# A mixture-of-experts kernel: expert items sorted by the table, and a second TensorE loop with 128 moving columns instead of 160

## The chip, the cores and the metric

One core of one Trainium2 chip runs the whole program. The metric is the device time in microseconds (us) of one execution; the time of a kernel is the median of its runs. Engine names are those of the profile: PE is TensorE's matmul side and PEld its weight loads, DVE is VectorE, ACT is ScalarE, POOL is GpSimd, SP is SyncE, which issues the weight loads.

## The reference, cut to what matters

The layer computes, for 1024 tokens of width 1024, a normalization, an input projection, two kinds of attention, an output projection, and then a mixture of experts. The change touches the last part alone.

```python
logits = (h @ w_router + b_router)
top_val, top_idx = lax.top_k(logits, 4)          # 4 of 32 experts per token
gate = jax.nn.softmax(top_val, axis=-1)
...
gu = xblk @ w_gate_up[e] + b_gate_up[e]
g_lin = jnp.minimum(gu[:, :D_EXPERT], 7.0)
u_lin = jnp.clip(gu[:, D_EXPERT:], -7.0, 7.0)
act = g_lin * jax.nn.sigmoid(1.702 * g_lin) * (u_lin + 1.0)
y = act @ w_down[e] + b_down[e]                  # times its gate, added to the token's row
```

Each expert has three 1024x1024 float32 matrices (gate, up, down), 12.58 MB. There are 4096 token-expert pairs, 128 per expert on average. Evaluated on the reference's inputs, the router gives the 32 experts these counts of tokens, in order of the expert's number: 128, 122, 123, 140, 105, 142, 107, 120, 131, 126, 127, 114, 147, 126, 138, 121, 120, 131, 118, 108, 160, 136, 132, 101, 121, 139, 112, 124, 129, 146, 152, 150. Fourteen are over 128 and none is over 160.

## The kernel before, in words

**Items.** The last block of the program (from L1125) works in items. An item is one expert and up to `SL` = 160 of its tokens; an expert with more would get a further item. A table in on-chip memory (`table`) holds for each item the expert and the first position; it is built at run time from the counts, on DVE and PE (L1442 to L1460 and L1620 to L1633). The first 32 entries are the experts in the order of their numbers, so item 0 is expert 0, whose weights are loaded before the table is there. `count_items` (L1121) loads the number of items on every engine, and every engine runs a loop over all items but the last (`Fori(0, n_last)`), then a copy of the loop's body for the last one.

**Tokens.** Tokens are the moving side of each product. DVE's `choose` (L1373) marks the tokens of an item, PE's `find` (L1543) turns the marks into row numbers, DVE's `rows` (L1379) into indices, and POOL gathers the rows (L1181), 80 in each of two halves. PE turns them (`turn_x`, L1551), ACT copies the result as a high and a low float16 part (`x_split`, L1249). Places without a token point at spare rows behind the output and have a gate of zero.

**Weights.** An item's weights come in six chunks of 2 MB: chunks 0 and 1 are the halves of gate, 2 and 3 of up, 4 and 5 of down. Three raw buffers make a ring: SP issues the load of chunk m+3 when DVE has finished with chunk m (`item_loads`, L1137). ACT writes a chunk's high float16 part (`high_part`, L1244, the instruction is L1247), DVE its low part (`low_part`, L1409, the instruction is L1412), into a ring of three part buffers, which ACT may fill again when PE has used them. Chunks 6 and 7 are chunks 0 and 1 of the next item.

**Products.** For every 128x128 piece of a weight chunk, `product` (L1577) issues three matmuls (high by high, high by low, low by high), each with its own weight load and 160 moving columns. A chunk is 96 matmuls, an item 576. I call an item's six products G0, G1, U0, U1, D0 and D1. PE's order in an item (L1643) is G0, `find` of the next item, two turns of the previous item's result (`turn_y`, L1563), G1, two more, U0, U1, half of the next item's `turn_x`, D0, the other half, D1. G0 writes the banks that hold D1's result of the item before, so its first three tiles wait until ACT has copied three tiles of that result (`y_copy`, L1279).

**DVE's order** in an item (L1468): `shift`, `rows` of the next item, low part 2, three `gate_read`, low part 3, five `gate_read`, low part 4, `gate_act`, the activation (`activate`, `activate_low`, L1424 to L1438), low part 5, `bias`, low part 6, `choose`, low part 7. **ACT's order** (L1294): high part 2, y rows, high part 3, y rows, high part 4, sigmoids, high part 5, `up_read` with activation parts, half of `x_split`, high parts 6 and 7, the other half, `y_copy`. All engines take their instructions strictly in this written order.

Of the kernel before, what the change touches and what calls it, by code (L numbers as in the profile page):

```python
# [6 lines left out]
BF16 = mybir.dt.bfloat16  # L7
FP16 = mybir.dt.float16
I32 = mybir.dt.int32
ALU = mybir.AluOpType  # L10
# [12 lines left out]
def build_trunk(nc, x, norm1_g, w_in, sb_q_norm_g, sb_k_norm_g, sb_out_norm_g, hg_lb_logits,  # L23
# [14 lines left out]
    with ExitStack() as ctx:  # L38
# [847 lines left out]
        ITEMS = NE + T * TOPK // SL  # L886
# [124 lines left out]
        table = sb("table", [1, 2 * TAB + 2], I32)  # L1011
        MORE = MAXC - 1
        work = region_b[:, 8192 + 6 * D:8192 + 8 * D]
# [15 lines left out]
        code_e, thr, pos1 = take(1), take(MORE), take(MORE)  # L1029
        code16 = take(4).bitcast(BF16)  # L1030
        over = take(4).bitcast(BF16)[:, 0:MORE]
        hot = take((MORE * TAB + 1) // 2).bitcast(BF16)[:, 0:MORE * TAB].rearrange("p (c j) -> p c j", c=MORE)
# [8 lines left out]
        NP8 = 15  # L1041
# [82 lines left out]

        with nc.Block() as block:  # L1125
# [29 lines left out]
            def _(pool):  # L1155
# [16 lines left out]
                pool.tensor_copy(code16[:, 1:1 + MORE], thr).then_inc(s_p8, 3)  # L1172
# [164 lines left out]
            def _(dve):  # L1337
# [95 lines left out]
                def activate_low(i, q):  # L1433
# [16 lines left out]
                link(dve.scalar_tensor_tensor(out=pos1[0:NE, :], in0=bank[4][0:NE, 0:MORE], scalar=float(NE + 1), in1=over[0:NE, :],  # L1450
                                              op0=ALU.add, op1=ALU.mult))
                dve.tensor_tensor(hot[0:NE, :, :], iota[0:NE, 1:TAB + 1].unsqueeze(1).to_broadcast([NE, MORE, TAB]),
                                  pos1[0:NE, :].unsqueeze(2).to_broadcast([NE, MORE, TAB]), ALU.is_equal).then_inc(s_hot, 1)
                dve.tensor_scalar(table[:, 2 * TAB:2 * TAB + 1], bank[4][0:1, MORE:MORE + 1], float(NE), None, ALU.add)
                dve.tensor_scalar(table[:, 2 * TAB + 1:2 * TAB + 2], bank[4][0:1, MORE:MORE + 1], float(NE - 1), None, ALU.add)
# [3 lines left out]
                dve.tensor_copy(table[:, NE:TAB], bank[3][0:1, NE:TAB])  # L1459
                dve.tensor_copy(table[:, TAB:2 * TAB], bank[3][0:1, TAB:2 * TAB]).then_inc(s_table, 1)  # L1460
# [62 lines left out]
            def _(pe):  # L1523
# [53 lines left out]
                def product(out_ap, r, f, kk, k, hi, lo, first):  # L1577
# [5 lines left out]
                def gate(i, half):  # L1583
                    pe.wait_ge(s_lod, i * CH + (half + 1))
                    for f in range(KT):
                        if half == 0 and f % TPB == 0:
                            pe.wait_ge(s_dnc, i * 3 + (f // TPB + 1))
                        for kk in range(HK):
                            if f == 0 and kk == 0:
                                pe.wait_ge(s_xhi, i * 2 + (half + 1))  # L1590
                                pe.wait_ge(s_xlo, i * 2 + (half + 1))
                            mm = product(tile_at(0, f), half, f, kk, half * HK + kk, xT_hi, xT_lo, half == 0 and kk == 0 and f % TPB == 0)
                        mm.then_inc(s_g, 1)

                def up(i, half, last):
# [3 lines left out]
                    for f in range(KT):  # L1599
                        for kk in range(HK):  # L1600
                            mm = product(tile_at(3, f), (2 + half) % RING, f, kk, half * HK + kk, xT_hi, xT_lo,
# [3 lines left out]
                def down(i, half):  # L1605
                    pe.wait_ge(s_lod, i * CH + (4 + half + 1))
                    for k0, k1 in ((0, 2), (2, 4)) if half == 0 else ((0, 4),):
                        for f in range(KT):
                            if half == 0 and k0 == 0 and f % TPB == 0:
                                pe.wait_ge(s_gev, i * 8 + min(f + TPB, KT))  # L1610
                            for kk in range(k0, k1):
# [4 lines left out]
                                mm = product(tile_at(0, f), (4 + half) % RING, f, kk, k, aT_hi, aT_lo, k == 0 and f % TPB == 0)  # L1616
# [5 lines left out]
                pe.matmul(bank[4][0:NE, 0:MORE], lt16[0:NE, 0:NE], over[0:NE, :], start=True, stop=False, skip_group_check=True)  # L1622
# [65 lines left out]
```

## Time and profile before

| What | Value |
|---|---|
| median of 3 runs | 2249.86 us (2248.14 to 2250.61) |
| the profiled execution, its own time | 2252.61 us |
| its span in the trace | 2250.7 us |
| mean granted TensorE clock over the span | 0.964 |
| PE busy | 2116.3 us, 94% of the span |
| DVE busy | 1548.6 us, 69% |
| ACT busy | 1412.7 us, 63% |
| POOL busy | 604.2 us, 27% |
| moved by DMA | 489.40 MB, mean 217 GB/s |

Shares are averages over a program with very different stages: up to about 800 us the attention part runs, with few loads; from then on the items. A matmul's busy time includes its way through a pipeline, so the time from one to the next has to be taken from a run of many, not from the mean of one. A timeline row gives the start, the length up to the end of the last instruction it merges, the engine, the line and the operation, and in brackets how long the engine stood idle before it and what ended that.

### The profile page before, as it was taken

The page shows a single profiled execution, that of the slowest core. Times are in us where ns is not written, and L with a number is a line of the kernel's source. Part 1 is how long each engine was busy: PE and PEld are TensorE (multiplying, and loading weights), DVE is VectorE, ACT ScalarE, POOL GpSimd, SP SyncE. Part 2 cuts the span into 40 slices and gives each one's busy share as a digit, 9 for nine tenths or more (in the row PEclk, how much of TensorE's full clock was granted, in tenths as well). Part 3 has the DMA queues.
Part 4 walks back from the last instruction along what each step waited for, and adds up shares of the span by engine and source line. Part 5 has one row for each costly group of instructions (what it writes and reads, how often), then busy time and mean ns, then how long its engine had stood idle before and what let it go on. Part 6 is the DMA issues. An engine that isn't in the chain of part 4 may idle for free.

```text
span 2250.7 us, 59693 instructions
## 1 busy us (share of the span) xinstructions
PE 2116.3 (94%) x24537; PEld 1796.4 (80%) x24537; DVE 1548.6 (69%) x1933; ACT 1412.7 (63%) x1633; POOL 604.2 (27%) x379
## 2 busy tenths in 40 slices
PE   5999999999937958999999999999999999999998
PEld 3444864344813548999999999999999999999997
DVE  5331424444673247888888888888888888888886
ACT  4331315564263346787777778778777877877884
POOL 2221212222050122322332332242233224223221
PEclk7999999999958969999999999999999999999999
DMA  4111100000031267898898998989889898988987
GB/s 159 38 46 48 57 1 1 0 1 1 30 121 50 84 238 260 311 326 315 316 327 306 329 316 315 328 314 328 307 317 326 311 334 313 329 308 317 325 307 239
DMA packets 142564, 489.40 MB, mean 217 GB/s; under 512 B 12794, under 2 KB 27898, under 8 KB 142448
## 3 DMA queue, kind: packets, MB, share of 16 engines
q1 hardware_dynamic: 129648, 444.78, 54.0%
q0 software_dynamic: 12864, 43.88, 8.2%
q8 instruction: 38, 0.62, 0.1%
q14 instruction: 14, 0.11, 0.0%
HBM read 457.34 MB, written 35.52 MB: 219 GB/s over the span
## 4 chain that ended last, share of the span: by engine, by line
PE 57%; DVE 3%; DMA 2%; issue 1%; ACT 1%; POOL 0%; POOLq 0%; DVEq 0%; SPq 0%; ACTq 0%
PE banks L1580 52%; PE banks L1574 3%; DVE region_c L1412 2%; PE banks L1560 1%; DMA rows_out<-region_b 1%; PE banks L1547 1%; DMA region_d<-w_down_dram 0%; DMA region_b<-rows_out,region_d 0%; ACT region_b L1267 0%; DMA rows_out<-region_b,region_d 0%; DVE region_b L1438 0%; ACT region_b L1253 0%; ACT region_b L1263 0%; POOL rows_out L1185 0%; POOL region_b L1177 0%
## 5 line engine op out<-in xcount | busy, mean ns | idle before, releaser
L1580 PE MATMUL banks<-region_b,region_c 128*128 128x160 f16 x18432 | 1300.1, 233 | 8.6 <-DVE region_c L1412 5.9
L1580 PEld LDWEIGHTS banks<-region_b,region_c 128*128 128x128 f16 x18432 | 1281.3, 98 | 12.9 <-DVE region_c L1412 7.0
L1412 DVE TENSOR_TENSOR region_c<-region_a,region_c 128x4096 f16<-128x4096 f32 x128 | 565.5, 4418 | 28.5 <-ACT region_c L1247 14.4
L1247 ACT ACTIVATE region_c<-region_a 128x4096 f16<-128x4096 f32 x128 | 462.5, 3613 | 52.1 <-DMA region_a<-w_gate_up_dram 52.1
L1181 POOL DMA_INDIRECT region_b<-rows_h,region_d x64 | 294.3, 4598 | 35.8 <-issue 28.8
L1247 ACT ACTIVATE region_c<-region_d 128x4096 f16<-128x4096 f32 x64 | 231.5, 3618 | 100.6 <-DMA region_d<-w_gate_up_dram 63.8
L1412 DVE TENSOR_TENSOR region_c<-region_d,region_c 128x4096 f16<-128x4096 f32 x64 | 282.5, 4414 | 2.7 <-ACT region_c L1247 2.7
L1190 POOL TENSOR_TENSOR region_d<-region_d 80x1 f32<-80x1 f32 x96 | 20.2, 210 | 923.6 <-DVE region_d L1389 656.8
L345 PE MATMUL banks<-region_a,region_d 128*128 128x512 f16 x960 | 210.9, 382 | 7.8 <-POOL region_d L319 7.8
L345 PEld LDWEIGHTS banks<-region_a,region_d 128*128 128x128 f16 x960 | 94.6, 99 | 124.3 <-POOL region_d L319 8.2
L1276 ACT ACTIVATE region_b<-banks,region_d 80x512 f32<-80x512 f32 x128 | 80.4, 678 | 138.8 <-PE banks L1574 125.7
L265 ACT ACTIVATE region_d<-region_d 128x2048 f16<-128x2048 f32 x14 | 26.6, 1909 | 147.9 <-PE banks L345 114.2
L1185 POOL DMA_INDIRECT rows_out<-region_b,region_d x66 | 100.3, 1520 | 43.5 <-issue 22.4
L319 POOL TENSOR_TENSOR region_d<-region_d 128x2048 f16<-128x2048 f32 x14 | 57.0, 4074 | 201.3 <-ACT region_d L265 201.3
L400 DVE COPY region_b<-banks 128x512 f32<-128x512 f32 x32 | 22.1, 692 | 127.9 <-PE banks L345 127.9
L513 DVE TENSOR_SCALAR region_a<-banks 128x1024 f32<-128x1024 f32 (+3 forms) x48 | 46.0, 958 | 91.4 <-PE banks L581 60.7
L1284 ACT ACTIVATE region_b<-banks,b_dcur 128x160 f32<-128x160 f32 x256 | 79.9, 408 | 23.4 <-PE banks L1580 23.1
L1263 ACT ACTIVATE region_b<-banks,region_d 128x160 f32<-128x160 f32 x256 | 85.1, 386 | 13.9 <-PE banks L1580 13.9
L972 PE MATMUL banks<-region_c,region_a 128*128 128x512 f16 x256 | 80.6, 387 | 11.2 <-DVEq L949 10.2
L550 ACT ACTIVATE region_a<-banks 128x1024 f32<-128x1024 f32 (+3 forms) x48 | 38.9, 810 | 77.9 <-PE banks L595 76.5
L353 PE MATMUL banks<-region_d,region_a 128*128 128x256 f16 x768 | 84.0, 273 | 0.0
L353 PEld LDWEIGHTS banks<-region_d,region_a 128*128 128x128 f16 x768 | 75.1, 98 | 8.9
(246 smaller groups left out, 2214.9 us busy)
## 6 DMA issues: line engine op xcount, KB each, us to landing
region_a<-w_gate_up_dram SPq DMA_DIRECT2D x192, 1024.0 KB
region_d<-w_gate_up_dram SPq DMA_DIRECT2D x64, 1024.0 KB
region_a<-w_down_dram SPq DMA_DIRECT2D x64, 1024.0 KB
region_d<-w_down_dram SPq DMA_DIRECT2D x64, 1024.0 KB
region_d<-w_in_dram SPq DMA_DIRECT2D x14, 1024.0 KB, 5.0
region_b<-x_dram SPq DMA_DIRECT2D x8, 1024.0 KB, 8.7
region_c<-w_out_dram SPq DMA_DIRECT2D x8, 512.0 KB, 3.6
rows_out<-region_b SPq DMA_DIRECT2D x8, 512.0 KB, 2.7
```

The costliest lines, as they stand in the source:

```text
L345: mm = pe.matmul(bank[q][:, :], a, b, start=(k == 0 and j == 0), stop=(k == KT - 1 and j == 2))
L353: mm = pe.matmul(bank[q][:, tt * WC:(tt + 1) * WC], a, b, start=(k == 0 and j == 0), stop=(k == KT - 1 and j == 2))
L972: mm = pe.matmul(bank[half][:, :], a, b, start=(k == 0 and j == 0), stop=(k == KT - 1 and j == 2))
L1181: pool.indirect_dma_start(out=xg[:, h, :], out_offset=None, in_=rows_h2[:, :], in_offset=bass.IndirectOffsetOnAxis(ap=rows_get[:, h:h + 1] ...
L1185: pool.indirect_dma_start(out=rows_out[:, :], out_offset=bass.IndirectOffsetOnAxis(ap=rows_prev[:, h:h + 1], axis=0), in_=yrow[:, h, :], i ...
L1247: act.activation(part_hi[r], raw[r], ACT.Copy).then_inc(s_hi9, 1)
L1263: act.activation(u_all[:, f * SL:f * SL + SL], tile_at(3, f), ACT.Identity, bias=b_cur[:, KT + f:KT + f + 1]).then_inc(s_uev, 1)
L1276: act.activation(yrow[:, h, q * 512:q * 512 + 512], bank[Y_BANK[g]][0:HS, :], ACT.Copy, scale=gate_prev[:, h:h + 1]).then_inc(s_yrow, 1)
L1284: ins = act.activation(yT[:, f, :], tile_at(0, f), ACT.Identity, bias=b_dcur[:, f:f + 1])
L1412: dve.tensor_tensor(part_lo[r], raw[r], part_hi[r], ALU.subtract).then_inc(s_lod, 1)
L1574: mm = pe.transpose(bank[Y_BANK[g]][0:HS, d * P:d * P + P], yT[:, 4 * q + d, h * HS:h * HS + HS], ident[:, :])
L1580: mm = pe.matmul(out_ap, a, b, start=(first and s == 0), stop=(k == KT - 1 and s == 2), skip_group_check=True)
```

## The change

Both the table and PE's code change. The table now lists first expert 0 (its threshold is set to -1, so that it always counts) and the experts with over 128 tokens, then further items of experts with over 160, then the experts with 128 or fewer. It is built from eight kinds of entry instead of six, each with a product of its own, and `table` gets one more word, the number of wide items. PE loads that number (`count_wide`), runs a loop over the wide items with 160 moving columns, a second loop with 128, and the last item with 128. The tiles keep their distance of 160 columns, and all other engines keep their loops and their 160 columns, so that DVE and ACT read 32 columns per tile that a narrow item's products do not write. DVE's `choose` of item 1 now takes its expert from the table, after the wait for it.

```diff
-        ITEMS = NE + T * TOPK // SL
+        ITEMS = NE + T * TOPK // SL + 2
+        NARROW = P
...
+        KINDS = MORE + 2
...
+        def count_wide(eng):
+            return eng.value_load(table[0:1, 2 * TAB + 2:2 * TAB + 3], min_val=1, max_val=ITEMS - 2)
...
-                pool.iota(thr, [[SL, MORE]], base=SL, channel_multiplier=0, allow_small_or_imprecise_dtypes=True).then_inc(s_p8, 1)
-                pool.wait_ge(s_p8, 10)
+                pool.iota(thr[:, 1:MORE + 1], [[SL, MORE]], base=SL, channel_multiplier=0, allow_small_or_imprecise_dtypes=True).then_inc(s_p8, 1)
+                pool.memset(thr[:, 0:1], float(NARROW)).then_inc(s_p8, 1)
+                pool.wait_ge(s_p8, 11)
+                pool.affine_select(out=thr[:, 0:1], in_=thr[:, 0:1], compare_op=ALU.is_gt, fill=-1.0, base=0, pattern=[[0, 1]],
+                                   channel_multiplier=1).then_inc(s_p8, 1)
...
-                dve.tensor_tensor(over[0:NE, :], thr[0:NE, :], bank[3][0:NE, 0:1].to_broadcast([NE, MORE]), ALU.is_lt).then_inc(s_over, 1)
+                dve.tensor_tensor(over[0:NE, 0:MORE + 1], thr[0:NE, :], bank[3][0:NE, 0:1].to_broadcast([NE, MORE + 1]), ALU.is_lt)
+                dve.tensor_tensor(over[0:NE, MORE + 1:KINDS], thr[0:NE, 0:1], bank[3][0:NE, 0:1], ALU.is_ge).then_inc(s_over, 1)
...
-                link(dve.tensor_copy(table[:, 0:NE], iota[0:1, 0:NE]))
...
-                dve.tensor_scalar(table[:, 2 * TAB:2 * TAB + 1], bank[4][0:1, MORE:MORE + 1], float(NE), None, ALU.add)
-                dve.tensor_scalar(table[:, 2 * TAB + 1:2 * TAB + 2], bank[4][0:1, MORE:MORE + 1], float(NE - 1), None, ALU.add)
+                link(dve.tensor_copy(totals[0:1, :], bank[4][0:1, KINDS - 1:KINDS + 1]))
+                dve.tensor_copy(table[:, 2 * TAB + 2:2 * TAB + 3], totals[0:1, 0:1])
+                dve.tensor_scalar(past[0:1, :], iota[0:1, 0:TAB], totals[0:1, 1:2], float((MAXC - 1) * SL), ALU.is_ge, ALU.mult)
+                link(dve.scalar_tensor_tensor(out=n_all[0:1, :], in0=totals[0:1, 0:1], scalar=2.0, in1=totals[0:1, 1:2],
+                                              op0=ALU.add, op1=ALU.max))
+                dve.tensor_copy(table[:, 2 * TAB:2 * TAB + 1], n_all[0:1, :])
+                dve.tensor_scalar(table[:, 2 * TAB + 1:2 * TAB + 2], n_all[0:1, :], -1.0, None, ALU.add)
...
-                choose(1, 0)
                 dve.wait_ge(s_table, 1)
+                choose(dve.value_load(table[0:1, 1:2], min_val=0, max_val=NE - 1),
+                       dve.value_load(table[0:1, TAB + 1:TAB + 2], min_val=0, max_val=(MAXC - 1) * SL))
...
-                def product(out_ap, r, f, kk, k, hi, lo, first):
+                def product(tile, width, r, f, kk, k, hi, lo, first):
+                    out_ap, hi, lo = tile[:, 0:width], hi[:, :, 0:width], lo[:, :, 0:width]
...
-                with pe.Fori(0, n_last) as i:
-                    item(i, False)
-                item(n_last, True)
+                n_wide = count_wide(pe)
+                with pe.Fori(0, n_wide) as i:
+                    item(i, False, SL)
+                with pe.Fori(n_wide, n_last) as i:
+                    item(i, False, NARROW)
+                item(n_last, True, NARROW)
```

## Rows read from the trace of the kernel before

**Rows 1.** The page's first part: busy time of each engine.
```profile
PE 2116.3 (94%) x24537; PEld 1796.4 (80%) x24537; DVE 1548.6 (69%) x1933; ACT 1412.7 (63%) x1633; POOL 604.2 (27%) x379
```

**Rows 2.** The chain that ended last, two items: start, length, what.
```profile
1709.86 13.42 PE banks L1580 x192
...
1732.29 13.28 PE banks L1580 x192
...
1753.36 13.38 PE banks L1580 x192
```

**Rows 3.** Waits from 880 to 2180 us by engine: total us, times, longest.
```profile
PE banks L1580 <- DVE region_c L1412: 0.7, 4, 0.2
...
DVE region_d L1384 <- PE banks L1547: 107.0, 30, 3.6
...
ACT region_c L1247 <- DMA region_d<-w_gate_up_dram: 61.7, 30, 2.3
```

**Rows 4.** Windows: us; busy us of PE, PEld, DVE, ACT, POOL; clock, DMA share, GB/s.
```profile
1622.70:1666.20 43.50, 43.47 (x640) 43.31 (x640) 37.44 (x44) 33.91 (x38) 13.06 (x7) 1.00 0.91 319
```

**Rows 5.** The page's costliest groups: products with 160 and with 256 moving columns.
```profile
L1580 PE MATMUL banks<-region_b,region_c 128*128 128x160 f16 x18432 | 1300.1, 233 | 8.6 <-DVE region_c L1412 5.9
...
L353 PE MATMUL banks<-region_d,region_a 128*128 128x256 f16 x768 | 84.0, 273 | 0.0
```

**Rows 6.** Timeline of one item, 1709 to 1754 us.
```profile
1709.12 0.74 PE L1560 MATMUL banks<-region_d,region_b 80*128 80x80 f16 x16
...
1709.84 4.42 DVE L1412 TENSOR_TENSOR region_c<-region_a,region_c 128x4096 f16<-128x4096 f32 x1
1709.94 0.93 SPq L1062 DMA_DIRECT2D region_d<-w_gate_up_dram  x2
1709.94 3.62 ACT L1247 ACTIVATE region_c<-region_a 128x4096 f16<-128x4096 f32 x1 [1.57 <-DMA region_a<-w_gate_up_dram]
...
1714.64 1.82 ACT L1284 ACTIVATE region_b<-banks,b_dcur 128x160 f32<-128x160 f32 x6
...
1719.26 3.62 ACT L1247 ACTIVATE region_c<-region_d 128x4096 f16<-128x4096 f32 x1 [1.90 <-DMA region_d<-w_gate_up_dram]
...
1723.12 0.74 PE L1547 MATMUL banks<-values,region_b 128*80 128x6 bf16 x16
...
1723.99 0.17 DVE L1384 COPY region_d<-banks 80x12 f32<-80x12 f32 x1 [3.57 <-PE banks L1547]
...
1724.86 4.41 DVE L1412 TENSOR_TENSOR region_c<-region_d,region_c 128x4096 f16<-128x4096 f32 x1
...
1729.43 0.93 SPq L1062 DMA_DIRECT2D region_d<-w_down_dram  x2
...
1738.96 3.62 ACT L1247 ACTIVATE region_c<-region_d 128x4096 f16<-128x4096 f32 x1 [0.97 <-PE banks L1580]
...
1743.18 0.33 DVE L1427 TENSOR_SCALAR region_b<-region_b 128x320 f32<-128x320 f32 x1 [0.45 <-ACT region_b L1263]
...
1753.03 3.62 ACT L1247 ACTIVATE region_c<-region_a 128x4096 f16<-128x4096 f32 x1 [1.20 <-DMA region_a<-w_gate_up_dram]
```

**Rows 7.** One window of 1 us in that item, columns as in rows 4.
```profile
1729.00:1730.00 1.00, 1.00 (x17) 1.00 (x15) 1.00 (x4) 0.14 (x1) 1.00 (x1) 1.00 0.00 0
```

**Rows 8.** Timeline, 800 to 885 us: table's last write, first low part, first shift.
```profile
822.17 0.20 DVE L1460 CAST table<-banks 1x65 int32<-1x65 f32 x1
...
824.95 4.42 DVE L1412 TENSOR_TENSOR region_c<-region_a,region_c 128x4096 f16<-128x4096 f32 x1 [2.58 <-ACT region_c L1247]
...
852.27 0.17 DVE L1400 COPY region_d<-region_d 80x2 f32<-80x2 f32 x1 [15.06 <-DMA rows_out<-region_b,region_d]
```

**Rows 9.** Timeline of the end, 2140 to 2251 us.
```profile
2242.48 1.41 DVE L1519 SCALAR_TENSOR_TENSOR region_b<-banks,region_d,region_b 80x512 f32<-80x512 f32 x2 [11.36 <-DMA region_b<-rows_out,region_d]
```

**Rows 10.** Timeline and clock of the first item: products after pauses of PE.
```profile
857.99 14.86 PE L1580 MATMUL banks<-region_b,region_c 128*128 128x160 f16 x192 [3.34 <-DVE region_c L1412]
...
875.31 6.80 PE L1580 MATMUL banks<-region_b,region_c 128*128 128x160 f16 x96 [1.88 <-DVE region_b L1438]
```

More of the change, by code:

```diff
@@ L1040, in build_trunk @@
         s_gissue = sem("first_gather_issued")
-        NP8 = 15
+        NP8 = 17
         CH = 6
@@ L1581, in product, with gate @@
                     return mm
-                def gate(i, half):
+                def gate(i, half, width):
                     pe.wait_ge(s_lod, i * CH + (half + 1))
@@ L1591, in gate, with up @@
                                 pe.wait_ge(s_xlo, i * 2 + (half + 1))
-                            mm = product(tile_at(0, f), half, f, kk, half * HK + kk, xT_hi, xT_lo, half == 0 and kk == 0 and f % TPB == 0)
+                            mm = product(tile_at(0, f), width, half, f, kk, half * HK + kk, xT_hi, xT_lo, half == 0 and kk == 0 and f % TPB == 0)
                         mm.then_inc(s_g, 1)
-                def up(i, half, last):
+                def up(i, half, last, width):
                     pe.wait_ge(s_lod, i * CH + (2 + half + 1))
@@ L1615, in down @@
                                     pe.wait_ge(s_alo, i * 4 + (k // 2 + 1))
-                                mm = product(tile_at(0, f), (4 + half) % RING, f, kk, k, aT_hi, aT_lo, k == 0 and f % TPB == 0)
+                                mm = product(tile_at(0, f), width, (4 + half) % RING, f, kk, k, aT_hi, aT_lo, k == 0 and f % TPB == 0)
                             if k1 == 4:
@@ L1621, in _ @@
                 pe.wait_ge(s_over, 1)
-                pe.matmul(bank[4][0:NE, 0:MORE], lt16[0:NE, 0:NE], over[0:NE, :], start=True, stop=False, skip_group_check=True)
-                for c in range(MORE):
-                    mm = pe.matmul(bank[4][0:NE, c + 1:MORE + 1], ones16[0:NE, 0:NE], over[0:NE, c:c + 1].to_broadcast([NE, MORE - c]),
-                                   start=False, stop=(c == MORE - 1), skip_group_check=True)
+                pe.matmul(bank[4][0:NE, 0:KINDS], lt16[0:NE, 0:NE], over[0:NE, :], start=True, stop=False, skip_group_check=True)
+                for c in range(KINDS):
+                    mm = pe.matmul(bank[4][0:NE, c + 1:KINDS + 1], ones16[0:NE, 0:NE], over[0:NE, c:c + 1].to_broadcast([NE, KINDS - c]),
+                                   start=False, stop=(c == KINDS - 1), skip_group_check=True)
                 mm.then_inc(s_upto, 1)
                 pe.wait_ge(s_hot, 1)
-                for c in range(MORE):
+                for c in range(KINDS):
                     pe.matmul(bank[3][0:1, 0:TAB], code16[0:NE, 0:1], hot[0:NE, c, :], start=(c == 0), stop=False, skip_group_check=True)
                 for c in range(MORE):
-                    mm = pe.matmul(bank[3][0:1, TAB:2 * TAB], code16[0:NE, 1 + c:2 + c], hot[0:NE, c, :], start=False, stop=(c == MORE - 1),
+                    mm = pe.matmul(bank[3][0:1, TAB:2 * TAB], code16[0:NE, 1 + c:2 + c], hot[0:NE, c + 1, :], start=False, stop=(c == MORE - 1),
                                    skip_group_check=True)
@@ L1641, in _, with item @@
                 n_items, n_last = count_items(pe)
-                def item(i, last):
-                    gate(i, 0)
+                def item(i, last, width):
+                    gate(i, 0, width)
                     if not last:
```

35 lines of the change are left out of this document (18 added, 17 removed).

## The prediction

> **What bounds the kernel now.** The page's first part puts PE at 94% of the span, far ahead of DVE, ACT and POOL [rows 1]. That is an average, and a busy PE need not be the limit, so I look next at the chain that ended last. From 880 us on it is nearly all item products; the same place in two neighbouring items, D1 with G0 behind it, begins at 1709.86 and at 1753.36, a period of 43.50 us [rows 2]. The table of waits agrees: over 1300 us the products waited 0.7 us for their weights, while DVE waited 107.0 us (30 times 3.6) for PE's `find`, and ACT 61.7 us for loads [rows 3]. So PE sets the pace, and the reader should see how narrowly: in one item DVE is busy for 37.44 us, ACT for 33.91, and the DMA engines for 0.91 of 43.50, which is 39.6 us [rows 4]. The counts in the section on the reference, and the 18432 products = 32 times 576 [rows 5], say that there are 32 items. With expert 0 and the 14 experts over 128 tokens, 15 are wide after the change and 17 narrow.
>
> **PE's part of a narrow item.** 192 products of 160 columns take 13.28 us, 69.2 ns each [rows 2]. 768 of 256 columns, each with its own weight load too, take 84.0 us, 109.4 ns each [rows 5]. That is 0.42 ns per column, so 128 columns should take 55.8 ns: an item saves 576 times 13.4 ns = 7.7 us, and PE alone would need 43.5 - 7.7 = 35.8 us. Could the weight load set a floor between? The lower bound of the rows is 16 products of 80 columns with a weight load of 128 columns each: 0.74 us less the 0.20 that one lasts, over 15, is 36 ns [rows 6]. The upper bound is 69.2 ns, no gain. I take 55.8, since 160 and 80 columns both scale with the columns. The Trainium skill speaks against the change here: its page "TensorE: Matmul & The Clock Gate", section "Back-to-back issue gap", has a stream of weight load and matmul at about 81 ns each for 128 columns. By it a narrow item would cost 576 times 11.8 ns = 6.8 us more and the kernel about 2366 us; the trace disagrees already, since 160 columns with the same load run at 69.2 ns.
>
> **What is late next.** If PE needs 35.8 us, DVE's 37.4 and the loads come ahead of it. The order of work is fixed, so I follow the two loops that the next item hangs on, with the durations of rows 6.
>
> *Loop A, through chunk 2.* Its load is issued when low part 5 ends, at 1709.84, and ACT can start on it at 1719.26 (9.4 us). High part and step to DVE: 3.7. So low part 2 can start 13.1 us after D1's start; now it starts at 1724.86, 15.0 after. From there to the end of low part 5 (1753.2) are 28.4 us, of which PE's share goes: the 0.97 that ACT's high part 5 waits for U0, the 0.45 that the activation waits for ACT because of it, and I count 0.4 for shorter waits of the kind inside the activation. Loop A: 13.1 + 28.4 - 1.8 = 39.7 us.
>
> *Loop B, through chunk 7.* Chunk 5's load is issued at 1729.43; chunk 7 is used at 1753.03, and the DMA engines work without a pause between. That is 23.6. Behind it ACT does the high part and two x copies (1709.94 to 1714.64: 4.7) and three y copies (0.9), without which G0 can't start. Then G0, 96 times 55.8 ns = 5.4; `find` to DVE (1723.12 to 1723.99) 0.9; `rows` 0.9; low part 2 and the issue 4.6. Sum 41.0 us. Now the same loop is 42.3, inside 43.5. It may shrink by up to 1.1: the gather of the next item's rows moves up into chunk 4's time, and chunk 7 is issued some 0.8 us sooner after chunk 6, as a pause of the queue shows that it waits for issues, not for bandwidth [rows 7].
>
> So a narrow item takes between 39.7 and 41.0; I take 40.5, nearer the loop that is the longer. That saves 3.0 us in each of 16 items. The last one loads no chunks 6 and 7; I give it 2. PE then stands idle for 4 to 5 us of each narrow item, ahead of D0 and D1.
>
> **Start.** The table gains two kinds of entry (four small matmuls) and six small DVE instructions against one removed, at the 0.20 us of its last write at most [rows 8]; with the matmuls I count 1.5 us. It was written at 822.37 and DVE's next big step began at 824.95, when ACT's first high part was ready [rows 8]: a cover of 2.6 us. POOL's two more small instructions (again 0.2 each) come ahead of the clearing of the spare rows and its store. The first item then waits until 852.27 for two scatters behind that store [rows 8]; the store lies in SP's queue behind 6 MB of weight loads, so I take 0 and keep 0.4. The two values loaded before `choose` of item 1 and PE's `count_wide` are some 0.1 us each; `choose` is covered by G0, PE's by that same wait till 852 us. If all of the cover were gone the start would cost 2 us in all.
>
> **Loop change and end.** Entering the last item's own copy of the code costs PE nothing now; entering a second loop should not either, bounds 0 and 1 us. Table order only changes which expert's weights come when; the bytes are the same. The bound at the end is a gather of the last rows, released by DVE after the last low part; it is awaited until 2242.48 [rows 9], so a shorter last D1 brings nothing.
>
> **Sum.** 16 times 3.0 and 2 is 50 us, less 1 for start and loop change: 49. Against the profiled execution's 2252.6 us that is 2203.6; the median of the runs is 2.7 us lower, so I predict **2201 us**, own range 2190 to 2212 (per item 39.7 to 41.0, and the loop change).
>
> **Rivals.**
> (1) *The loads hold more than I think.* If the DMA engines' 39.6 busy us don't shrink and half of the 3.9 us without traffic stays (the wait for low part 5, ahead of chunk 2), an item takes 41.6: saving 17 times 1.9 = 32, time 2218; with scatters in the way of chunk 2 up to 2230. For it: a share of 0.91 [rows 4]. Against it: pauses with nothing in flight [rows 7]. Chance 0.20.
> (2) *DVE alone sets the pace.* Loads land earlier once they are issued more evenly, and an item takes 37.4 + 1 of waits = 38.5: 85 us less, 2165 (PE's own floor would give 2119). Against it: ACT already waits 2 us per item for chunk 2 [rows 3]. Chance 0.10.
> (3) *No gain*, because the weight load's pace is 69 ns or the sort puts nothing into the narrow loop (the change doesn't do what it says): 2250. The rows with 80 and 256 columns speak against the first, the counts against the second. Chance 0.04.
> (4) *Slower: the clock falls.* PE now runs without pauses and the granted clock is 1.00 [rows 4]. After a pause of 3.34 us in the first item, 192 products took 14.86 us, not 13.45; after one of 1.88 us, 96 took the usual 6.80 [rows 10]. A narrow item has pauses of about 2.6 us (before D0) and 1.4 (before D1). If each cost 1.4 us, PE would need 38.6 us and nothing changes; it decides only from 7.7 us lost per item, 144 products at half the clock. With half of the products there (288 times 53 ns = 15.3), an item takes 51 and the kernel 17 times 7.6 = 129 us more, 2379. Chance 0.03.
>
> **How the numbers follow.** My case has 0.63, the rivals 0.20, 0.10, 0.04 and 0.03. The range of 8 in 10 takes my case and most of (1) and part of (2): 2176 to 2225. What this kernel's measurement can tell from no change is about 0.2%, 4.5 us. Faster: my case, (1) and (2), 0.93. Same: (3), 0.04. Slower: (4), 0.03.
>
> **What would show it.** Right: 9792 products with 128 columns (17 times 576) and 8640 with 160; 96 of 128 columns in about 5.4 us; periods of 43.5 us in the first 15 items and 40 to 41 afterwards; `find` no longer awaited for 3.6 us by DVE; new waits of PE before D0 and D1 for DVE; a granted clock still at 1.00; the first item's G1 and U0 where they were. Wrong: products 69 ns apart (3), the DMA share near 1.00 and ACT's waits for chunks grown (1), wide items slower than 43.5, or a clock below 1 in the narrow part (4).

## The result and the profile after

The changed kernel takes 2218.91 us (median of 4 runs, 2216.3 to 2220.97) against 2249.14 for the kernel before beside it: a ratio of 0.9866, with an interval of 0.9851 to 0.9882. That is faster by 30 us. The range of 8 in 10 (2176 to 2225) held it, the likeliest case's own range (2190 to 2212) did not: 48 us were forecast. It came out at the time worked out for rival (1), 2218.

The profiled execution took 2216.3 us, with a span of 2214.5, so 2.6 us under the median, where the one of before lay above its own. Its page first, the busy engines and the costliest groups:

```profile
PE 2010.8 (91%) x24541; PEld 1685.8 (76%) x24541; DVE 1547.2 (70%) x1937; ACT 1409.8 (64%) x1633; POOL 610.6 (28%) x381
...
L1190 POOL DMA_INDIRECT region_b<-rows_h,region_d x64 | 298.8, 4668 | 35.8 <-issue 28.8
```

PE lost 105 us of work [rows 1], DVE and ACT next to none (1.4 and 2.9 us), and the kernel gained less than a third of that. The line of the products is L1596 now; with its shapes kept apart (busy us, mean ns, idle before it):

```profile
L1596 PE MATMUL banks<-region_b,region_c 128*128 128x160 f16 x8640 | 611.6, 233 | 6.9 <-DVE region_b L1447 2.9 <-issue 2.1 <-DVE region_c L1421 1.2
L1596 PE MATMUL banks<-region_b,region_c 128*128 128x128 f16 x9792 | 579.3, 223 | 65.3 <-DVE region_b L1447 37.4 <-ACT region_b L1293 18.7 <-DVE region_c L1421 9.0
```

9792 products are narrow and 8640 wide, so 17 items and 15. Of the 72 us that PE waits ahead of products, 65 lie in the narrow items. The chain that ended last has a wide item, a narrow one in which the clock was low for a while (products at 1732.37, granted clock 0.64 on average over them), and two narrow ones at the full clock:

```profile
1054.39 13.46 PE banks L1596 x192
...
1732.37 8.32 PE banks L1596 x96
...
1741.27 5.36 PE banks L1596 x96
...
1787.92 5.52 PE banks L1596 x96
...
1811.27 12.13 DMA region_a<-w_gate_up_dram
...
1829.39 5.52 PE banks L1596 x96
```

In the wide part the chain was all products; now a load of some 12 us stands in most narrow items, and in a few one of 8 us for chunk 5. The period of a narrow item is 1829.39 - 1787.92 = 41.47 us. From `find` to `find` the 14 last narrow periods take 41.42 on average, two at the change of loops 42.4 and 42.5, and the first 12 wide ones 43.60, against 43.50 for the same 12 before. One wide window and two narrow ones, columns as in rows 4:

```profile
1100.00:1143.50 43.50, 43.50 (x645) 43.48 (x643) 37.76 (x45) 34.13 (x38) 13.05 (x7) 1.00 0.90 321
1751.00:1793.00 42.00, 37.06 (x657) 36.48 (x655) 37.42 (x44) 34.62 (x38) 13.27 (x7) 1.00 0.95 339
1793.00:1835.00 42.00, 36.87 (x655) 36.29 (x653) 37.44 (x44) 34.38 (x38) 13.39 (x7) 1.00 0.96 336
```

The wide one is that of [rows 4] again. In the narrow ones no engine is full, and the DMA share rose to 0.95 or 0.96: times 41.4 that is some 39.6 us of DMA work per item, what it was. The waits from 880 to 2150 us (total, times, longest):

```profile
DVE region_d L1393 <- PE banks L1562: 89.4, 30, 4.9
...
ACT region_c L1256 <- DMA region_d<-w_gate_up_dram: 54.9, 30, 2.8
ACT region_c L1256 <- DMA region_a<-w_gate_up_dram: 45.6, 30, 2.7
...
PE banks L1596 <- DVE region_b L1447: 34.6, 16, 3.1
...
ACT region_c L1256 <- DMA region_d<-w_down_dram: 25.5, 14, 3.3
...
PE banks L1596 <- ACT region_b L1293: 17.1, 14, 1.6
```

Beside [rows 3]: PE now waits for DVE's activation in every narrow item (ahead of D0) and, which was not forecast, for ACT's y copies (ahead of G0). ACT's waits for the half of `w_down` that is chunk 5 grew to 25.5 us; in the kernel before the same view has 7.9 us for them, in 6 waits from 880 to 2180. DVE still waits for `find`. One narrow item in the timeline, from low part 2 to the next low part 2:

```profile
1795.12 4.42 DVE L1421 TENSOR_TENSOR region_c<-region_d,region_c 128x4096 f16<-128x4096 f32 x1
1795.65 4.72 POOL L1190 DMA_INDIRECT region_b<-rows_h,region_d  x1 [0.57 <-issue]
...
1799.71 0.93 SPq L1065 DMA_DIRECT2D region_d<-w_down_dram  x2
...
1808.63 3.62 ACT L1256 ACTIVATE region_c<-region_d 128x4096 f16<-128x4096 f32 x1 [1.76 <-DMA region_d<-w_down_dram]
...
1815.01 5.52 PE L1596 MATMUL banks<-region_b,region_c 128*128 128x128 f16 x96 [2.12 <-DVE region_b L1447]
...
1822.57 5.53 PE L1596 MATMUL banks<-region_b,region_c 128*128 128x128 f16 x96 [1.46 <-DVE region_c L1421]
...
1822.67 0.93 SPq L1065 DMA_DIRECT2D region_d<-w_gate_up_dram  x2
1823.49 3.62 ACT L1256 ACTIVATE region_c<-region_a 128x4096 f16<-128x4096 f32 x1 [2.38 <-PE banks L1596]
...
1828.18 2.39 ACT L1293 ACTIVATE region_b<-banks,b_dcur 128x160 f32<-128x160 f32 x8
...
1829.39 5.52 PE L1596 MATMUL banks<-region_b,region_c 128*128 128x128 f16 x96 [1.29 <-ACT region_b L1293]
...
1834.74 0.74 PE L1562 MATMUL banks<-values,region_b 128*80 128x6 bf16 x16
...
1835.62 0.17 DVE L1393 COPY region_d<-banks 80x12 f32<-80x12 f32 x1 [2.46 <-PE banks L1562]
...
1836.59 4.42 DVE L1421 TENSOR_TENSOR region_c<-region_d,region_c 128x4096 f16<-128x4096 f32 x1
```

Both loops of the prediction can be measured here. Through chunk 7 (loop B of the prediction): issue of chunk 5 to high part 7, 1823.49 - 1799.71 = 23.8; to the start of the y copies 4.7; to G0 1.2 (three copies, and 0.24 until PE starts); to `find` 5.35; to DVE 0.9; `rows` 1.0; low part 2 and the issue 4.6: together 41.5, the item. (That high part names PE as what it waited for; PE's products were long done, and the chain has the load, 1811.27 and 12.13 us, ending there.) Through chunk 2 (loop A): 13.2 from the end of low part 5 to that of high part 2, then 27.4 from low part 2 to the end of low part 5: 40.6. Third is the DMA work, 39.6. Three limits lie within 2 us.

In time the change is this: 14 narrow periods less 2.1 each is 29.4, two of 1.0, the wide ones give back 1.2 in all, behind the last `find` 2.7, and the first shift comes 4 us sooner, at 848.00, of which 3 reach the first items [rows 8]. That is 36, the difference of the spans. The last 3 are the run's and not the change's: the kernel of run e8 below, which has no sort, has its first shift at 847.88.

```profile
823.07 4.43 DVE L1421 TENSOR_TENSOR region_c<-region_a,region_c 128x4096 f16<-128x4096 f32 x1 [0.40 <-issue]
...
848.00 0.17 DVE L1409 COPY region_d<-region_d 80x2 f32<-80x2 f32 x1 [13.96 <-DMA rows_out<-region_b,region_d]
```

### The profile page after: what moved, and what is told of

Same layout as the page of the kernel before. It is cut to its first block, busy times and chain, and to the rows that moved or that the text cites. A ratio compares the mean times of both kernels' runs of the same rounds, so it can differ in the third digit from the quotient of the medians.

```text
span 2214.5 us, 59720 instructions
## 1 busy us (share of the span) xinstructions
PE 2010.8 (91%) x24541; PEld 1685.8 (76%) x24541; DVE 1547.2 (70%) x1937; ACT 1409.8 (64%) x1633; POOL 610.6 (28%) x381
## 4 chain that ended last, share of the span: by engine, by line
PE 31%; DMA 11%; DVE 10%; issue 8%; ACT 2%; SPq 0%; POOL 0%; DVEq 0%; ACTq 0%; POOLq 0%
PE banks L1596 28%; DVE region_c L1421 8%; DMA region_a<-w_gate_up_dram 7%; DMA region_d<-w_down_dram 2%; PE banks L1589 1%; DVE region_b L1426 1%; DMA rows_out<-region_b 1%; DMA region_d<-w_gate_up_dram 1%; PE banks L1562 1%; PE banks L1575 1%; ACT region_b L1262 1%; ACT region_b L1260 0%; SPq L1065 0%; DMA region_b<-rows_out,region_d 0%; ACT region_b L1293 0%
## 5 line engine op out<-in xcount | busy, mean ns | idle before, releaser
L1596 PE MATMUL banks<-region_b,region_c 128*128 128x128 f16 (+1 forms) x18432 | 1190.8, 228 | 72.1 <-DVE region_b L1447 40.3
L1596 PEld LDWEIGHTS banks<-region_b,region_c 128*128 128x128 f16 x18432 | 1171.6, 99 | 80.0 <-ACT region_b L1276 42.3
L1190 POOL DMA_INDIRECT region_b<-rows_h,region_d x64 | 298.8, 4668 | 35.8 <-issue 28.8
```

Source lines behind the costliest of these rows:

```text
L1190: pool.indirect_dma_start(out=xg[:, h, :], out_offset=None, in_=rows_h2[:, :], in_offset=bass.IndirectOffsetOnAxis(ap=rows_get[:, h:h + 1] ...
L1596: mm = pe.matmul(out_ap, a, b, start=(first and s == 0), stop=(k == KT - 1 and s == 2), skip_group_check=True)
```

## The experiments

What had to be told apart: is the narrow item held by its order (the loop through chunk 7), by the loads' bytes, by a clock that was granted at 0.96 of full in most narrow items, or does the sort cost something of its own? Each kernel was timed beside the kernel before. Edits are to the changed kernel unless said.

**e1, sort alone.**

```diff
-                    item(i, False, NARROW)
-                item(n_last, True, NARROW)
+                    item(i, False, SL)
+                item(n_last, True, SL)
```

> The change without its narrow products: the table is sorted and PE has its second loop, but both loops use 160 moving columns; the result is the reference's. If the sort, the larger table and the second loop cost next to nothing, as the prediction has it, the time is 2249 us within 3, and an item takes 43.5 us in both loops. If the 0.2 us that each wide item grew by in the changed kernel (43.7 against 43.5) come with the new code and not with the narrow items, all 32 items take 43.7 here and the time is 2252 to 2256 us, unless the start is shorter by the 3 us that it is in the changed kernel's profile.

Measured: 2251.51 us against 2248.97, ratio 1.0012 [1.0003, 1.0022]. The first shift came at 847.03, and an item of its second loop has the window of [rows 4]:

```profile
1676.43:1719.94 43.51, 43.51 (x643) 43.37 (x641) 37.58 (x44) 33.93 (x37) 13.12 (x7) 1.00 0.92 320
```

So table, sort and second loop cost 2.5 us, by the interval between 0.7 and 4.9; the gain is that of the columns alone.

**e2, 96 columns.** As e1's diff, with 96 in place of `NARROW`.

> The change with 96 instead of 128 moving columns in the narrow loop; tokens past the 96th of a narrow item are left out of the products. Theory A (the loop through chunk 7: loads of chunks 5 to 7, high part, x copies, y copies, G0, find, rows, low part 2): only G0's saving lies in the loop, 96 times 13.3 ns = 1.3 us, until the loop through chunk 2 (40.6 us in the changed kernel's trace) takes over: narrow items 40.6 instead of 41.4, time 2205 within 4. Theory B (the DMA engines' 39.6 us of work per item and a pause that stays): nothing changes, 2219. Theory C (PE still bounds, by its own speed or its clock): 7.7 us less per narrow item, below 2110.

Measured: 2232.84 us, 0.9921 [0.9901, 0.9941]: slower than with 128 columns, by 14 us. PE has less to do than with 128 columns, and most items are longer, 39.9 to 47.3 us, with a lower mean clock (0.926). Here is one of them:

```profile
1884.00:1928.50 44.50, 30.17 (x644) 29.35 (x641) 37.33 (x45) 33.72 (x37) 12.95 (x7) 0.88 0.90 308
```

PE is idle for 14 of 44.5 us, no engine is full, and the DMA share is down. Something gets in the way when PE is early.

**e3, the y copy first.** G0 waits for this copy; it is put ahead of an x copy that has time.

```diff
                         high_part(7, i * 64 + 96)
+                    y_copy(i, 0)
+                    if not last:
                         x_split(i + 1, 1)
-                    for b in range(3):
+                    for b in range(1, 3):
                         y_copy(i, b)
```

> The change with one move in ACT's order: the first y copy (three tiles of the down product, on which the next item's G0 waits) stands ahead of the second half of the x copies instead of behind it; the result is the reference's. Theory A: G0 starts 1.4 us sooner after chunk 7 has landed, the loop through chunk 7 takes 40.1 us, the one through chunk 2 (40.6) takes over: narrow items 40.6, time 2205 within 4. Theory B: an order on ACT does not change what the DMA engines have to move, 2219. Wide items stay at 43.5 to 43.7 under both.

Measured: 2232.09 us, 0.9931 [0.9914, 0.9948]. In most narrow items `find` does come 1.3 us sooner, at 10.8 us after low part 5 in place of 12.1, and yet the items take 40.2 to 44.0, most over 42, and the kernel is 13 us slower than the changed one.

**e4, half of chunk 4's bytes.** It leaves half of each row of chunk 4 (a quarter of `w_down`) unloaded.

```diff
-                sp.dma_start(raw[r][:, 2 * q:2 * q + 2, :], src).then_inc(s_raw[r], 16)
+                w = D // 2 if m == 4 else D
+                sp.dma_start(raw[r][:, 2 * q:2 * q + 2, 0:w], src[:, :, 0:w]).then_inc(s_raw[r], 16)
```

> The change with half of chunk 4's load left out (columns 512 to 1023 of the first half of the down matrix stay what the buffer held), 1.05 MB less per item. Chunk 4 lands before chunk 5 is issued, so it lies outside the loop through chunk 7. Theory A: narrow items stay at 41.4 within 0.3, time 2219 within 5. Theory B: at the 420 GB/s that the DMA engines reach, 2.5 us less work per item, narrow items about 39, or 40.6 if the loop through chunk 2 holds them, time 2180 to 2205.

Measured: 2217.3 us, 0.9857 [0.984, 0.9875], the same as the changed kernel within the spread of either. A narrow item:

```profile
1875.07:1916.27 41.20, 36.32 (x644) 35.76 (x641) 37.43 (x44) 33.85 (x38) 13.40 (x7) 1.00 0.91 313
```

The DMA work fell to 37.5 us and the item stayed at 41.2. So with the order as it is, the total of the bytes does not hold it; a loop does, in which chunk 4 has next to no part, as its load is all but over when chunk 5 is issued.

**e5, filler.** 36 small products that nothing uses fill PE's pause ahead of D0, to keep the clock up.

```diff
+                    if width < SL:
+                        pe.wait_ge(s_gev, i * 8 + TPB)
+                        for _ in range(36):
+                            pe.matmul(bank[0][:, 0:P], ident16, ident16, start=True, stop=True, skip_group_check=True)
                     down(i, 0, width)
```

> The change with 36 extra matmuls of 128 columns (2.0 us) in each narrow item, on a constant and into a bank that D0 overwrites, where PE otherwise waits 2.1 us before D0; the result is the reference's. In the changed kernel's trace 13 of the 17 narrow items have a stretch at the lower clock (granted clock 0.96 or 0.92 over the item). Theory A (the loop through chunk 7 sets the pace, and the clock's losses lie in PE's slack): the granted clock of the narrow items rises to 1.00, their length stays at 41.4, time 2218 within 4. Theory D (the clock's falls lengthen the narrow items): they become shorter, below 41, time under 2210.

**e6, e3 and e5 together.**

> The run with the y copy moved ahead of the x copies, with the same filler before D0. There, items with a granted clock of 1.00 took 40.2 us and those with a lower one 41 to 44. Theory A with the clock as a second limit: with the clock kept at 1.00 all narrow items take 40.2, time 2249 less 17 times 3.2 = 2197 within 4. If the clock was only a companion of the long items and not their cause, they stay between 40 and 44 and the time at 2225 to 2235.

Measured: e5 2224.11 us, 0.9896 [0.9866, 0.9927]; e6 2230.35, 0.9913 [0.9896, 0.9929]. The clock was granted in full in most items of e5 and nothing was won; its runs spread from 2217.6 to 2230.4 us, and the profiled one took 2219.1. In e3 the short items (40.2) had a clock of 1.00 and the long ones 0.92 or 0.96, which made the clock a suspect; but in e6 items at a clock of 1.00 take up to 42.3 us, so the clock is not e3's cause. In the changed kernel too, items with a clock of 1.00 (41.3 to 41.5) and of 0.92 (41.6) are alike. But e5 is the run that points to the cause of e3's loss, for its items come in two lengths at one clock:

```profile
1668.39:1710.53 42.14, 38.02 (x680) 37.72 (x678) 37.79 (x44) 33.64 (x38) 11.53 (x7) 1.00 0.93 329
1877.34:1918.55 41.21, 38.34 (x679) 37.73 (x677) 37.44 (x44) 33.70 (x38) 13.36 (x7) 1.00 0.95 338
```

POOL is busy for 11.5 us in the long one and for 13.4 in the short one. The timeline of a long item of e5, at low part 2:

```profile
1668.39 0.74 PE L1562 MATMUL banks<-values,region_b 128*80 128x6 bf16 x16
...
1670.76 0.94 POOL L1190 DMA_INDIRECT region_b<-rows_h,region_d  x1 [0.57 <-issue]
1670.87 4.42 DVE L1421 TENSOR_TENSOR region_c<-region_d,region_c 128x4096 f16<-128x4096 f32 x1 [0.56 <-ACT region_c L1256]
1672.01 4.08 POOL L1190 DMA_INDIRECT region_b<-rows_h,region_d  x1 [0.30 <-issue]
...
1678.93 3.62 ACT L1256 ACTIVATE region_c<-region_a 128x4096 f16<-128x4096 f32 x1 [1.79 <-DMA region_a<-w_down_dram]
```

and of the first short one behind it, in the same execution. (Short is meant from low part 5 to low part 5, 41.1 us against 42.1 for the long one shown; from `find` to `find` it takes 41.96, as the next `find` comes 0.9 later behind its low part 5.)

```profile
1752.70 0.74 PE L1562 MATMUL banks<-values,region_b 128*80 128x6 bf16 x16
1754.87 4.42 DVE L1421 TENSOR_TENSOR region_c<-region_d,region_c 128x4096 f16<-128x4096 f32 x1 [0.25 <-ACT region_c L1256]
1755.07 5.04 POOL L1190 DMA_INDIRECT region_b<-rows_h,region_d  x1 [0.57 <-issue]
...
1761.95 3.62 ACT L1256 ACTIVATE region_c<-region_a 128x4096 f16<-128x4096 f32 x1 [0.51 <-DMA region_a<-w_down_dram]
```

POOL's first gather comes 2.4 us after `find`. Where it is ahead of low part 2, by 0.11 us, it goes out in 0.94 us, and the second takes until low part 2 is over. Where it is behind, by 0.20 us, it takes until low part 2 is over (1759.29) and 0.8 more, and the second the same with low part 3. The rows themselves move about 3 us after that, and share the DMA engines with the weights, as the profile's count by queue shows. In the long item the first gather's rows go from 1674.6 to 1677, while chunk 4 is in flight: from 1674 to 1677 us the weights' queue moved 0.71 MB beside 0.33 of the gather, 0.24 MB per us, and alone, from 1677.5 to 1679, 0.41 MB per us. Chunk 4's high part waits 1.8 us for the load and comes 10.9 us after the issue, against 9.7. In the short item next to nothing of the gather moves before 1763, when chunk 4 is down. The loop that grows is the one through chunk 2: in e5's five items with an early gather low part 4 starts 0.6 us later behind low part 3, and from low part 5 to low part 5 they take 42.3 on average, the nine with a late one 41.3. The same holds in e3 (seven at 42.6, seven at 41.2) and in e6 (twelve at 42.4, two at 41.2). The changed kernel always has the second kind (the gather at 1795.65, 0.5 behind low part 2). There the load of chunk 4 is over when chunk 5 is issued, at 1799.71, as windows of 1 us show, and the rows follow from 1803.5 to 1806, in chunk 5's time:

```profile
1798.00:1799.00 1.00, 1.00 (x21) 1.00 (x19) 1.00 (x1) 1.00 (x1) 1.00 (x1) 1.00 1.04 418
1799.00:1800.00 1.00, 1.00 (x22) 1.00 (x19) 1.00 (x3) 0.35 (x1) 1.00 (x1) 1.00 0.50 201
1800.00:1801.00 1.00, 1.00 (x15) 0.99 (x12) 1.00 (x3) 0.24 (x1) 0.69 (x2) 1.00 0.61 102
```

Why a gather beside a low part takes so long has a rule in the Trainium skill, page "SBUF — State Buffer", section "SBUF: two separate sides": DVE, with two inputs in SBUF, and a POOL operation that reads SBUF lock one pair of ports between them for a whole instruction; whoever comes first has it, and the other stands still. The trace agrees for POOL: 0.94 us for a gather that came first, 4.7 to 5.0 for one behind. That DVE stands still behind POOL it doesn't show: low part 2 takes 4.42 us in both items.

**e7, 128 columns in every item.** The tokens past 128 of a wide item are left out.

```diff
-                    item(i, False, SL)
+                    item(i, False, NARROW)
```

> The change with 128 moving columns in the first loop too; tokens past the 128th of a wide item are left out of the products. Theory A: all 32 items take 41.4 instead of 43.5, time 2249 less 32 times 2.05 = 2183 within 6, so the gain follows the number of narrow items. If part of the gain of the changed kernel were from the start or from the order of the experts, it would be less.

Measured: 2191.26 us, 0.975 [0.9726, 0.9773], 8 us more than expected: 58 us for 32 items, 1.8 each, items of 41.1 to 42.0 and two of 42.6 and 43.1. The gain per narrow item is near the 2.1 of the changed kernel, so the bulk of it hangs neither on the order of the kinds nor on which experts come late.

**e8, the move of e3 in the kernel before.**

> The kernel before the change, with the first y copy ahead of the second half of the x copies and nothing else changed; the result is the reference's. Theory A: with 160 columns PE sets the pace and the loop through chunk 7 has 1.3 us of slack, so the move changes nothing: 2249 within 3. If the move itself brought something, it would show here as well.

Measured: 2250.92 us, 1.0007 [0.9997, 1.0016]. Where PE sets the pace, the move does nothing: the items keep their 43.4 to 43.6 us.

**e9, e3 with a late gather.** The gather waits for high part 2 of the next item as well.

```diff
                         pool.wait_ge(s_sel1, i + 2)
+                        pool.wait_ge(s_hi9, i * CH + 3)
```

> The run with the y copy moved, and in it POOL's gather of the next item's rows waits in addition for high part 2, so that it goes out with low part 2 as it does in the changed kernel. Theory E (the gather): where G0 is early, rows is ready up to 1 us before low part 2 can start, both gathers go out at once (0.9 us each on POOL instead of 4.7) and their rows take the DMA engines from chunk 4, whose high part then starts at 21.4 us after low part 5 instead of 19.9, and the item takes 42. With the gather held back all narrow items take 41.0 or less, time 2207 within 5. Theory D (the clock): the gather does not matter, the long items stay, time 2225 to 2235.

Measured: 2228.4 us, 0.991 [0.9883, 0.9936]. The time is the one expected if the gather did not matter (2225 to 2235), and yet it does. High part 4 was back at 20 us after low part 5, where it comes at 21.2 or later in e3's items with an early gather (in which only the first half goes out at once; the second takes 4.0 to 4.4 us), and ten of the narrow items took 40.3 to 41.6, mostly under the changed kernel's. That the gather was what held chunk 4 up is shown by this edit, which moves nothing else. But five items took 42.4 to 46.2, because chunk 5 came late. In the longest:

```profile
1798.88 4.34 POOL L1199 TENSOR_TENSOR region_d<-region_d 80x1 f32<-80x1 f32 x1 [19.58 <-ACT region_c L1257]
...
1803.33 0.93 SPq L1065 DMA_DIRECT2D region_d<-w_down_dram  x2
1803.37 0.95 POOL L1190 DMA_INDIRECT region_b<-rows_h,region_d  x1
...
1817.87 3.62 ACT L1257 ACTIVATE region_c<-region_d 128x4096 f16<-128x4096 f32 x1 [6.57 <-DMA region_d<-w_down_dram]
```

Chunk 5 took 14.5 us, 8.9 being usual. The gather doesn't explain it: its two halves are over 1.0 and 5.8 us after chunk 5's issue, against 0.7 and 5.8 in the changed kernel. The first row is a sum of 80 elements, 0.2 us elsewhere, that took until low part 2 was over.

**e10, e3 and e4 together.**

> The run with the y copy moved, with half of chunk 4's load left out (those columns of the first half of the down matrix stay what the buffer held). Half a chunk alone brought nothing in the changed kernel, and the moved y copy alone made it slower. Theory E: with chunk 4 half as long the gather no longer delays it, the narrow items take 40.2 to 41, time 2203 within 6. Theory D: no change against the run with the y copy moved, 2232.

Measured: 2208.4 us, 0.9827 [0.9809, 0.9845], 10 us under the changed kernel; most items 40.1 to 41.0, about the sum of the loop through chunk 2, 40.6. Neither half of this did anything good alone. Against e4 only the y copy has moved, and the runs of the two don't overlap (2213.3 to 2217.9 us there, 2207.3 to 2213.1 here): the 9 us between the medians are what the shorter loop through chunk 7 is worth once chunk 4 is out of the way. Low part 2 now waits 0.50 us for ACT's high part 2 (second row below), so it is the loop through chunk 2 that sets the pace. The gathers go out early, as in e3, but with chunk 4 short its high part awaits nothing:

```profile
1953.36 0.95 POOL L1191 DMA_INDIRECT region_b<-rows_h,region_d  x1 [0.57 <-issue]
1953.41 4.42 DVE L1424 TENSOR_TENSOR region_c<-region_d,region_c 128x4096 f16<-128x4096 f32 x1 [0.50 <-ACT region_c L1257]
...
1959.62 3.61 ACT L1257 ACTIVATE region_c<-region_a 128x4096 f16<-128x4096 f32 x1
```

**e11, e2 with the late gather of e9.**

> The run with 96 moving columns in the narrow loop (the rest of an item's tokens left out of the products), with the gather held back until high part 2 is ready. Theory E: the items of 42 to 47 us there are those in which find came 9 to 11 us after low part 5 and the gather took the time of chunk 4; held back, all take 41 or less and the time is 2207 within 6, though PE is idle for as long as before and its clock as low. Theory D: PE's idle time and so the clock's falls are the same, and the time stays at 2232.

Measured: 2223.79 us, 0.9906 [0.9873, 0.9939]. The median is 9 us under e2's, with the mean clock as low as there (0.930), but the runs of the two overlap (2220 to 2238 and 2227 to 2240), and neither 2207 nor 2232 was met. Two thirds of the items take 39.8 to 41.8, the rest up to 45.5. This fits with a part of e2's loss hanging on when the gather goes out, but doesn't show it, and the lengths that remain are not explained.

**e12, half of chunk 6's bytes.** It leaves half of each row of the next item's chunk 0 unloaded: the chunk that goes through the queue behind chunk 5 and ahead of the one that G0 needs.

```diff
-        def load(sp, e, m):
+        def load(sp, e, m, first=True):
...
-                sp.dma_start(raw[r][:, 2 * q:2 * q + 2, :], src).then_inc(s_raw[r], 16)
+                w = D if first or m != 0 else D // 2
+                sp.dma_start(raw[r][:, 2 * q:2 * q + 2, 0:w], src[:, :, 0:w]).then_inc(s_raw[r], 16)
...
-                        load(sp, e if m < RING else e_next, (m + RING) % CH)
+                        load(sp, e if m < RING else e_next, (m + RING) % CH, False)
```

> The change with half of chunk 6's load left out (columns 512 to 1023 of the first half of the gate matrix stay what the buffer held, but for item 0). It is the same 1.05 MB per item that the run with half of chunk 4 left out, but here between the issue of chunk 5 and the landing of chunk 7. Theory A (the loop through chunk 7 sets the narrow items' pace): up to 2.5 us less in that loop, the loop through chunk 2 takes over, narrow items 40.7 instead of 41.4 and the time 2207 within 4, where half of chunk 4 gave 2217. If the amount moved did not matter in either place, 2218 as in the changed kernel.

Measured: 2226.75 us, 0.9888 [0.9872, 0.9905]; a miss. Fewer bytes in the loop through chunk 7 should have shortened it. They did bring `find` forward, to 11 us after low part 5 in most items, and of the six items in which chunk 5 was used within 9.6 us of its issue five took 39.9 to 41.3. But four others took 44.1 to 47.3 us. In the one from 1800 to 1845 us chunk 5 is used 12.8 us after its issue, in the next 15.0, and the gathers of the first went out late and blocked, as in the changed kernel. An early gather is thus not the only thing that makes a load late, and this run does not settle what the loop through chunk 7 is worth; e10 beside e4 does.

## Why the prediction was right and wrong

**Right.** PE's own pace: 96 products of 128 columns in 5.36 us (5.52 with the tail), 55.8 ns each, as forecast from the rows of 160 and 256 columns; the 81 ns of the Trainium skill ("TensorE: Matmul & The Clock Gate", "Back-to-back issue gap") do not hold here, with a weight load for every product. The counts, 17 and 15. The new waits ahead of D0 and D1 (2.1 and 1.5 us). Start: no cost beyond the 2.5 us of e1, which has the second loop too. The end is bound by a gather of the last rows, as in [rows 9], so a shorter last D1 brought nothing. And that the order of work, through chunk 7, is the longest loop, with 41.0 as its plain sum: e4 takes work off the DMA engines outside of it and gains nothing, e10 shortens it beside e4 and gains 9 us. Of the signs named for this case two did not come: the clock was granted at 0.96 in most narrow items, and DVE still waits for `find`, 3.0 us on average. The loop through chunk 7 runs through `find`, so by the prediction's own reasoning that wait had to stay.

**The step that failed** is the allowance on that loop, "may shrink by up to 1.1", by which 40.5 was taken for an item in place of 41.0. The issue of chunk 5 to high part 7 was counted at 23.6 and took 23.8; the y copies at 0.9 and took 1.2, as the 0.24 until PE starts were left out; `rows` 0.9 and 1.0. That is 0.5 more than 41.0 where up to 1.1 less was hoped for. The allowance had two grounds. The first was the gather moving up into chunk 4's time. e5 shows in one execution what happens if it does: the item is some 0.9 longer, for chunk 4 then lands late. In the changed kernel it does not move up, since low part 2 keeps POOL waiting. The second was that chunk 7 is issued 0.8 us sooner after chunk 6. It is, 5.8 us in place of 6.6, but from chunk 5's issue to high part 7 the narrow items take 23.7 on average as the items before did: with the DMA engines busy for 0.94 of that time in the item shown, the sooner issue only waits longer.

In the profiled executions the forecast missed by 12.7 us (2203.6 against 2216.3). 16 items of 0.9 are 14.4, the two at the change of loops 2.2 more, the wide ones 1.2; the end and the allowance for start and loop change give back 1.7 and the earlier start 3, which is no merit of the change, as e8 has it too. The other 5 of the 18 us between forecast and measured gain are the distances of the two profiled executions from their medians.

**Also missed:** the loop through chunk 2 holds a wait for chunk 5's load, used 13.5 us behind low part 2, and took 40.6 where 39.7 was counted. It doesn't set the item, but it is about the floor that e10 reached, so the low end of the likeliest case's range was out of reach.

**Rival (1)** had the right size, 41.6 for 41.4, and half the reason. The DMA work did stay at 39.6 us and its share rose to 0.95. But e4 took 2 us of that work away and got nothing, so bandwidth alone is not the limit; e10 shows that the same bytes count once the order lets them. It is a chain of loads, each started by a step of DVE, and hardly a pause is left in it. That the time fell on rival (1)'s 2218 is in part luck, then: its 41.6 came from a pause that stays, not from the loop. **Rival (2)**, DVE alone at 38.5, was met by no item of any kernel. **Rival (3)** fell with the 55.8 ns and the counts. **Rival (4)**: the clock did fall, to 0.96 and once 0.92 of full over an item, and 96 products then took up to 8.32 us; but the loss lay in PE's 4 to 5 us of slack, and the items kept their length. e5, which kept the clock at 1.00 in most items, won nothing.

**What stays open.** Why chunk 5 takes 13 to 15 us in single items of e2, e9, e11 and e12 (12 to 13 in e3 and e6), with early gathers and with late ones; what e2 loses besides; and whether 40.5 can be had with all bytes loaded. No version tried with all of the work in it beats the changed kernel: e3 2232, e5 2224, e6 2230, e9 2228 us.

## What to carry to other kernels

When the engine that bounds is relieved by more than the distance to the next limit, work out the next loop by its instructions and take its plain sum; an allowance for things that will fall into place needs a row of its own. Here three limits (two loops of dependences and the DMA work) lay within 2 us, and then no single edit made the kernel faster: e4 did nothing alone and e3 harm, and together they gained 10 us. And after an engine is made early, look at which transfers its results set off, for an early one can land in a worse place.

## What the runs showed of the hardware

- **Three tenths of a microsecond decide 4 us of POOL's.** A gather issued by POOL 0.11 us ahead of a big fp32 step of DVE takes 0.94 us, one 0.20 us behind it takes 5.04, and the item is 42.1 or 41.1 us long by it, from low part 5 to low part 5. Even a POOL sum of 80 elements took 4.34 us in place of 0.2. The block was a help here, as it kept the rows' traffic out of chunk 4's time.
- **Two DMA queues share the engines.** While the rows of a gather moved, the weights' queue moved 0.24 MB per us; alone, right after, 0.41.
- **The clock fell without cost.** In narrow items, with pauses of 1 to 2.5 us ahead of G0, D0 and D1, the grant fell from 2.4 to 1.2 GHz for short stretches: 1.00 became 0.96 or 0.92 over an item, and 96 products took up to 8.32 us (mean grant 0.64) in place of 5.52. With 96 columns the items had 0.82 to 0.92. The time of the item showed none of it in the changed kernel.
- **Loads do not come at one speed.** Chunk 5, 2 MB, took some 8.9 us from issue to use in the changed kernel's narrow items and up to 15.0 in single items of e12, at the same place of the order.
